# An encoder trunk on eight cores: the tail of the retention group norm is reordered, and half of the state's bf16 copies move to GpSimd

## What is computed

```python
def step(state, qkv):                       # one chunk, one direction
    qi, ki, vi = qkv
    scores = jnp.einsum('bhid,bhjd->bhij', qi, ki) * intra_decay
    out = jnp.einsum('bhij,bhjv->bhiv', scores, vi)
    out = out + jnp.einsum('bhid,bhdv->bhiv', qi * q_decay, state)
    state = state * chunk_decay + jnp.einsum('bhjd,bhjv->bhdv', ki * k_decay, vi)
    return state, out
...
o = o_fwd + o_bwd
o = o - jnp.mean(o, axis=-1, keepdims=True)                       # group norm, per token and head
o = o * lax.rsqrt(jnp.mean(o * o, axis=-1, keepdims=True) + NORM_EPS)
return (jax.nn.silu(g) * o.astype(x.dtype)) @ w_o
```

## Time and profile before

| | us |
|---|---|
| two runs | 4858.53 and 5156.21, median 5007.37 |
| the profiled execution | 4702.69 |
| its span, slowest core (7) | 4701.6 |
| spans of all cores | 4670.8 to 4701.6 |
| mean granted TensorE clock of the cores | 0.916 to 0.923 |
| busy, core 7: PE / DVE / ACT / POOL | 3935.8 / 1492.5 / 1539.7 / 1039.7 |

### The profile page before, as it was taken

One profiled execution on the slowest core, in us unless ns is written; L12 is line 12 of the kernel. 1 busy time (PEld: TensorE's weight loads), 2 busy tenths in 40 slices (PEclk: granted clock), 3 DMA queues, 4 the chain that ended last, 5 costly groups with the idle time before them and its releaser, 6 DMA issues.

```text
span 4701.6 us, 57281 instructions; the slowest of 8 cores (4670.8 to 4701.6 us)
## 1 busy us (share of the span) xinstructions
PE 3935.8 (84%) x17553; PEld 1719.2 (37%) x17553; DVE 1492.5 (32%) x2537; ACT 1539.7 (33%) x2739; POOL 1039.7 (22%) x946
## 2 busy tenths in 40 slices
PE   3666798999989999999867678879798897978879
PEld 2222343443434444444323233334343343433334
DVE  3102324334242525243243042341513324142341
ACT  2111233433242433334234134152432515144141
POOL 3121020202112020202133223212322222223122
PEclk8778898999999999999978899999999999999999
DMA  9999856455454545445698953344434444444333
GB/s 133 148 151 170 187 161 177 168 176 161 171 179 163 187 155 191 162 170 166 194 207 165 160 174 124 144 148 153 157 118 171 127 154 145 137 159 132 135 110 126
DMA packets 262929, 742.01 MB, mean 158 GB/s; under 512 B 105950, under 2 KB 144862, under 8 KB 204268
## 3 DMA queue, kind: packets, MB, share of 16 engines
q1 hardware_dynamic: 132172, 679.63, 44.5%
q0 software_dynamic: 130464, 58.73, 12.9%
HBM read 692.16 MB, written 163.58 MB: 182 GB/s over the span
## 4 chain that ended last, share of the span: by engine, by line
PE 64%; issue 8%; DVE 7%; DMA 7%; ACT 6%; another core or an unknown queue 4%; POOL 3%; SPq 0%; DVEq 0%; ACTq 0%; POOLq 0%
PE bank L427 46%; PE bank L653 5%; PE bank L725 4%; DMA sb_wring<-wscr 4%; PE bank L886 3%; ACT sb_Sbf L575 2%; DVE sb_xn L419 1%; PE bank L413 1%; DVE sb_misc L948 1%; PE bank L566 1%; DMA wscr<-w_down 1%; PE bank L943 1%; POOL sb_hm L855 1%; PE bank L939 1%
## 5 line engine op out<-in xcount | busy, mean ns | idle before, releaser
L427 PE MATMUL bank<-sb_xn,sb_wring 128*128 128x512 bf16 x5120 | 1254.4, 403 | 199.5 <-DVE sb_xn L419 75.1
L427 PE MATMUL bank<-sb_hm,sb_wring 128*128 128x512 bf16 x4608 | 1021.9, 384 | 59.2 <-DMA sb_wring<-wscr 26.6
L451 POOL TENSOR_TENSOR sb_hm<-sb_rstd 128x512 bf16<-128x512 f32 x512 | 529.5, 1039 | 1705.8 <-ACT sb_rstd L450 1704.1
L427 PEld LDWEIGHTS bank<-sb_xn,sb_wring 128*128 128x128 bf16 x5120 | 516.1, 102 | 924.5 <-issue 419.7
L427 PEld LDWEIGHTS bank<-sb_hm,sb_wring 128*128 128x128 bf16 x4608 | 454.6, 99 | 623.2 <-issue 96.7
L450 ACT ACTIVATE sb_rstd<-bank 128x512 f32<-128x512 f32 x512 | 302.5, 596 | 762.4 <-PE bank L427 581.5
L653 PE MATMUL bank<-sb_xn,sb_wring 128*128 128x512 bf16 x1536 | 375.9, 403 | 42.8 <-DMA sb_wring<-wscr 29.4
L569 DVE SCALAR_TENSOR_TENSOR sb_S<-sb_S,bank 128x512 f32<-128x512 f32 x512 | 312.5, 679 | 301.3 <-PE bank L566 289.3
L403 ACT ACTIVATE sb_xn<-sb_xT 128x512 bf16<-128x512 f32 x224 | 134.8, 629 | 621.1 <-DVE sb_xT L463 424.3
L463 DVE TENSOR_TENSOR sb_xT<-bank,sb_xT 128x512 f32<-128x512 f32 x96 | 66.4, 691 | 767.0 <-PE bank L427 767.0
L575 ACT CAST sb_Sbf<-sb_S 128x512 bf16<-128x512 f32 x512 | 292.3, 618 | 29.4 <-DVE sb_S L569 14.5
(11 more groups left out here) (168 smaller groups left out, 3020.3 us busy)
## 6 DMA issues: line engine op xcount, KB each, us to landing
sb_wring<-wscr SPq DMA_DIRECT2D x400, 1024.0 KB, 5.8
sb_wring<-wscr SPq DMA_DIRECT2D x64, 768.0 KB, 5.7
sb_scr<-sb_Sbf SPq DMA_DIRECT2D x32, 1024.0 KB, 8.8
sb_kvA<-sb_scr SPq DMA_DIRECT2D x128, 256.0 KB, 3.7
sb_xin<-x SPq DMA_DIRECT2D x32, 512.0 KB, 10.3
wscr<-w_up POOLq DMA_DIRECT2D x16, 1024.0 KB, 94.1
wscr<-w_down POOLq DMA_DIRECT2D x32, 512.0 KB, 37.2
x_scr<-sb_xT SPq DMA_DIRECT2D x8, 2048.0 KB, 7.8
```

The costliest lines, as they stand in the source:

```text
L427: PE.op(lambda: nc.tensor.matmul(bk[:], slab[:, k * C + mm * 128:k * C + (mm + 1) * 128], rhs[k], start=(k == 0), stop=(k == KC - 1)), rea ...
L451: POOL.op(lambda: nc.gpsimd.tensor_tensor(hm_k[j], rt, rt, ALU.mult), reads=[rstd_R[rb]], writes=[HR[j]])
```

## The change

Three things. The group norm of a head is finished at once, in the loop, and not one head later. The shift nm is computed in two steps: DVE negates the mean (nmn, by a tensor_scalar of one column) right behind the aggregate, and ACT multiplies it with rs (an Identity activation with a pointer scale); rs and nm now have a region of their own, `misc_R[8 + h]`. And in pass 2 `state_update` gives the casts of dc = 1 (odd i) to POOL; pass 1 keeps all on ACT.

```diff
--- before.py
+++ after.py
@@ -558,7 +558,7 @@
                   reads=[rot_R[2], rot_R[3]], writes=[rot_R[2]])
             emit2(rot[:, 2, :], rot_R[2])
 
-        def state_update(n, kt, ktR, vt_c, vt_cR, gC, sbuf_i, boundary, grp="main"):
+        def state_update(n, kt, ktR, vt_c, vt_cR, gC, sbuf_i, boundary, grp="main", split_copy=False):
             for h in range(4):
                 for dc in range(2):
                     i = h * 2 + dc
@@ -572,8 +572,12 @@
                     if boundary:
                         DVE.op(lambda: nc.vector.tensor_scalar(S[:, i, :], S[:, i, :], flag_ap, None, ALU.mult),
                                reads=[S_R[i], R_const], writes=[S_R[i]])
-                    ACT.op(lambda: nc.scalar.copy(Sbf[:, sbuf_i, i, :], S[:, i, :]),
-                           reads=[S_R[i]], writes=[Sbf_R[sbuf_i][i]])
+                    if split_copy and dc == 1:
+                        POOL.op(lambda: nc.gpsimd.tensor_copy(Sbf[:, sbuf_i, i, :], S[:, i, :]),
+                                reads=[S_R[i]], writes=[Sbf_R[sbuf_i][i]])
+                    else:
+                        ACT.op(lambda: nc.scalar.copy(Sbf[:, sbuf_i, i, :], S[:, i, :]),
+                               reads=[S_R[i]], writes=[Sbf_R[sbuf_i][i]])
 
         GCF = [math.exp(128.0 * LGF[h]) for h in range(4)]
         GCB = [math.exp(128.0 * LGB[h]) for h in range(4)]
@@ -913,22 +917,6 @@
                        reads=[bsR, R_const], writes=[PT_R[pb]])
                 gb_ = c % 2
                 STAGE[0] = "P2.ret.o"
-                obanks = []
-
-                def gn_finish(h, c=c, gb_=gb_, obanks=obanks):
-                    bo, boR = obanks[h]
-                    ag = misc[:, 32 + 4 * h:32 + 4 * h + 2]
-                    rs_ = misc[:, 32 + 4 * h + 2:32 + 4 * h + 3]; nm = misc[:, 32 + 4 * h + 3:32 + 4 * h + 4]
-                    mR = misc_R[h]
-                    DVE.op(lambda: nc.vector.scalar_tensor_tensor(nm, ag[:, 0:1], -1.0, rs_, ALU.mult, ALU.mult),
-                           reads=[mR], writes=[mR])
-                    ob = h % 2
-                    ACT.op(lambda: nc.scalar.activation(on_[ob], bo[:], AF.Identity, bias=nm, scale=rs_),
-                           reads=[boR, mR], writes=[rot_R[ob]])
-                    POOL.op(lambda: nc.gpsimd.tensor_tensor(gated[:, 4 * gb_ + h, :], on_[ob],
-                                                            gact[:, c, h * 512:(h + 1) * 512], ALU.mult),
-                            reads=[rot_R[ob], gact_R[c][h]], writes=[gated_R[gb_][h]])
-
                 for h in range(4):
                     bo, boR = bank("o")
                     PE.op(lambda: nc.tensor.matmul(bo[:], PTb[:, h * 128:(h + 1) * 128], v2[:, h * 512:(h + 1) * 512],
@@ -942,21 +930,26 @@
                         m = 2 * h + dc
                         PE.op(lambda: nc.tensor.matmul(bo[:], qb_k[m][:, cs_], sbl[:, m, :], start=False, stop=(dc == 1)),
                               reads=[qb_R[m], sbl_R[h]], writes=[boR], signal=(dc == 1))
-                    st = misc[:, 8 * h:8 * h + 6]; ag = misc[:, 32 + 4 * h:32 + 4 * h + 2]
-                    rs_ = misc[:, 32 + 4 * h + 2:32 + 4 * h + 3]
-                    mR = misc_R[h]
+                    st = misc[:, 8 * h:8 * h + 6]; nmn = misc[:, 8 * h + 6:8 * h + 7]
+                    ag = misc[:, 32 + 4 * h:32 + 4 * h + 2]
+                    rs_ = misc[:, 32 + 4 * h + 2:32 + 4 * h + 3]; nm = misc[:, 32 + 4 * h + 3:32 + 4 * h + 4]
+                    mR = misc_R[h]; mR2 = misc_R[8 + h]
                     DVE.op(lambda: nc.vector.bn_stats(st, bo[:]), reads=[boR], writes=[mR])
                     DVE.op(lambda: nc.vector.bn_aggr(ag, st), reads=[mR], writes=[mR])
-                    ACT.op(lambda: nc.scalar.activation(rs_, ag[:, 1:2], AF.Ln, bias=EPS, scale=1.0), reads=[mR], writes=[mR])
-                    ACT.op(lambda: nc.scalar.activation(rs_, rs_, AF.Exp, scale=-0.5), reads=[mR], writes=[mR])
-                    obanks.append((bo, boR))
-                    if h >= 1:
-                        gn_finish(h - 1)
-                gn_finish(3)
+                    DVE.op(lambda: nc.vector.tensor_scalar(nmn, ag[:, 0:1], -1.0, None, ALU.mult), reads=[mR], writes=[mR])
+                    ACT.op(lambda: nc.scalar.activation(rs_, ag[:, 1:2], AF.Ln, bias=EPS, scale=1.0), reads=[mR], writes=[mR2])
+                    ACT.op(lambda: nc.scalar.activation(rs_, rs_, AF.Exp, scale=-0.5), reads=[mR2], writes=[mR2])
+                    ACT.op(lambda: nc.scalar.activation(nm, rs_, AF.Identity, scale=nmn), reads=[mR, mR2], writes=[mR2])
+                    ob = h % 2
+                    ACT.op(lambda: nc.scalar.activation(on_[ob], bo[:], AF.Identity, bias=nm, scale=rs_),
+                           reads=[boR, mR2], writes=[rot_R[ob]])
+                    POOL.op(lambda: nc.gpsimd.tensor_tensor(gated[:, 4 * gb_ + h, :], on_[ob],
+                                                            gact[:, c, h * 512:(h + 1) * 512], ALU.mult),
+                            reads=[rot_R[ob], gact_R[c][h]], writes=[gated_R[gb_][h]])
                 if n + 1 < NCH:
                     ret_loads_sb(n + 1)
                 STAGE[0] = "P2.ret.st"
-                state_update(n, kf2, kf2_R, v2, v2_R, GCF, 0, boundary=(n == 15), grp="r")
+                state_update(n, kf2, kf2_R, v2, v2_R, GCF, 0, boundary=(n == 15), grp="r", split_copy=True)
                 STAGE[0] = "P2.ret.gT"
                 for half in range(2):
                     bk, bR = bank("r")
```

## The result

| | before | after |
|---|---|---|
| median of all runs | 4763.96 us (32 runs, 4686.15 to 5274.12) | 4671.67 us (33 runs, 4657.04 to 5218.8) |
| profiled execution | 4702.69 us | 4674.73 us |
| span of the slowest core | 4701.6 us | 4673.7 us |

The ratio of the undisturbed runs is 0.9945, with a 95% interval of 0.9927 to 0.9962; in part of the executions of either kernel the cores of one die run at a lower granted clock and the time is up to 12% longer, so the medians of all runs mix two levels and the ratio doesn't. The change gains 0.55%, about 26 us; the profiled executions differ by 28.0 us. That is far from 2%, and clear of no change.

What follows compares the result with a forecast made beforehand. Bound: a chain over four engines in pass 2's retention chunks. Eight tiles at 1.5 us give 12, slow-clock chunks 3.5, tile 0 hides 1: about 15 us, 4702.69 to 4688 profiled, scaled 5007.37 to 4991; range 4690 to 5110.

Steps and rivals of the forecast that it cites:

- part (3): Plain chunk: nmn3 waits for gate1 on POOL through the shared port; updates start at T 7.70, chunk 13.53 us, 0.34 gained.
- rival A: nmn does not wait for POOL: plain chunk 13.14 us, 0.73 gained; 27 us in all, 4676 profiled; chance 0.23.
- The chain: Plain chunk's period: updates from T 8.04, 4.79 to the next mask, 1.04 to the next matmul, sum 13.87 us.
- the casts: State casts on ACT: the next chunk does not wait for them, except in the last chunk of a tile.
- part (1): Norm of each head: nm moves to ACT as an Identity with pointer scale, taken as a step of 0.40 us.
- part (4): After gate3, ending T 10.93, next chunk's scores are ready some T 12.1 against 12.49 on DVE's side, covered by 0.4.
- part (5): Four of eight state casts go to POOL: 0.7 us each, all in time, worth nothing in a plain chunk.
- rival C: Slower: POOL copies bind from 1.7 us each; at 2.2 us plain chunk 14.6, 5034 us in all; chance 0.09.
- part (6): Last chunk of a tile: wo projection starts at T 13.75 instead of 14.68, 0.93 us gained on ACT.
- part (7): First chunk of a tile: overlap hiding its table load is lost; updates at 8.97 against 8.81, 0.1 to 0.2 us lost.
- part (8): Chunk at lower clock: updates at about T 8.75 instead of 9.79, 1.0 us gained; five such chunks give 3.5 more.
- Tile 0: First tile: PE waits 21 us for a load there, which hides 1 us of the gain.

## Why the prediction was right or wrong

The sign was right, and so was that the change stays within 2%. Two steps failed: the low end of the range, so that the measured median lies outside it, and the port wait of part (3). The change gained 26 to 28 us where the sum had 15; of the 11 to 13 between them, part (3) makes some 8 (0.32 us in each of 16 plain chunks, 0.33 in each of 8 last ones), the first chunks 1, the clock 2 to 3.

- **The range failed by its scale.** I carried the forecast over in proportion to the median of the two runs then shown, 5007.37 us. Over 32 runs the median before is 4763.96, and the two runs both lie well above it. In proportion to the profiled execution the forecast was 4688, rival A 4676; measured were 4674.73 profiled and 4671.67 in the median. The low end of 4690 lay above even my own sum for the profiled execution: with a profile that had run 6% faster than the median, the low end had to go below that sum.
- **The port wait, part (3), failed.** I let nmn3 wait for gate1, since the 512-column operation did. It doesn't wait, in any of the 52 of 128 cases in which it starts beside a gate. The runs with two columns and with two inputs show what does wait, and that even then I had mis-sized the term: 0.12 us a chunk, not 0.56. Of the 0.44 between them, 0.24 is that the unheld updates start at T 7.38 and not 7.14, with nmn3 at 7.21 and not 7.04, when gate1 (T 6.40 to 7.55) is nearly over; 0.20 is that behind a held nmn3 they start at 7.5 and not 7.70. So of the 0.32 by which a plain chunk came out shorter than forecast, 0.12 is the wait that wasn't there, and 0.20 its length.
- **Rival A had the right mechanism** (chance given 0.23): 0.73 a plain chunk there, 0.66 measured; 27 us in all there, 26 measured by the ratio. That the sums agree so well is in part luck. It had the updates at T 7.1 and the mask waiting for the scores; they start at 7.38, and at full clock the mask doesn't wait. It had 0.25 for the first chunk and 1.45 for the last, where 0 and 1.26 came out, and the clock made up for that.
- **The chain, and the casts, held.** 4.79 and 1.04 are unchanged; with the split undone the plain chunk doesn't move, and with the split alone it doesn't either.
- **nm on ACT, part (1), held, at its upper end.** It takes 0.294 us, and from its start to the apply's are 0.44 us where I had 0.40. With it head 3 came at 4.71 (4.62 forecast). The rest of the 0.24 is 0.07 from PE to the statistics and 0.07 to the first update.
- **What is late next, part (4), was close.** In a plain chunk of after at full clock the mask finds the scores ready, 0.24 us ahead of it in the chunk shown (they end at 4486.62); at a lower clock it waits for them. With the updates made early the scores bind, as the run with four banks shows.
- **The copies on POOL, part (5), held:** 0.57 us each in a row (0.7 taken), all in time. The threshold of 1.7 is bracketed by 1.15 and 2.3. The price behind it was far above mine: rival C had a plain chunk of 14.6 at 2.2 us a copy, measured are 16.6 to 17.8 at 2.3.
- **The last chunk, part (6),** gained 1.26, not 0.93, since the updates were not held: rival A's 1.45 less the longer steps.
- **The first chunk, part (7):** a loss of 0.1 to 0.2 was forecast. In tile 4 the median over the cores went from 14.62 to 14.80 and the updates from T 8.77 to 8.96 (8.97 forecast), and over seven tiles the mean is unchanged. Head 3 came at 5.92 (5.90 forecast). But the hit is in part luck: nmn3 isn't held here either (0.15 us); instead the statistics of head 3 come 1.5 to 1.9 behind its first matmul in tile 4 (1.4 to 1.6 before, 1.34 forecast), since the matmuls between them run in part at a lower clock (two take up to 1.06 us instead of 0.59). The gain that rival A had here, without the wait, didn't come.
- **Clock, part (8).** At full clock the chain gives 2 x 0.66 + 1.26 = 2.6 us a tile, 18 over seven tiles, and chunk 15's extra 5.8 us became 5.5. The seven tiles lost 25.3 on core 7 and 23.8 in the mean of the cores. So some 18 us are the chain's, and 5 to 7 come from fewer or cheaper chunks at the lower clock. I had 0.7 more for each of five such chunks, 3.5. That the shorter idle times bring it isn't shown: with the split alone some 5 us beyond the last chunks came too, at unchanged plain chunks, and in the four-bank run the clock fell.
- **Tile 0** gave nothing on core 7; there the load is the bound. I had taken off 1 us for this, and left it 0.5.

## What to carry to other kernels

Lay a stage's chain out by one period and check that its parts add up to the period before pricing a change: here the 4.79 from the first update to the mask and the 1.04 to the next matmul held wherever the scores were ready, and a longer distance showed that the other chain had taken over. Two edits that each cut one of two nearly equal chains give little or nothing alone and much together, and an edit that takes a wait off one engine may only pay with the order that another engine needs for it; try such edits in pairs. And when the level of the times is uncertain, let the range reach below the sum for the fastest execution seen.

## What the runs showed of the hardware

- A DVE operation that starts beside a POOL tensor_tensor was held to within 0.03 us of its end if it had two SBUF inputs (scalar_tensor_tensor of one column, up to 1.06 us instead of 0.16) or was a tensor_scalar of two columns (up to 1.04 instead of 0.17); a tensor_scalar of 512 columns took 1.47 instead of 0.49 beside one. Not held were a tensor_scalar of one column (0.153 to 0.156 us in all 128 cases, 52 of them beside a gate), the aggregate (six columns in, two out, 0.181 to 0.183), and the state updates, which read PSUM and one SBUF tensor (0.60 a step). The Trainium skill ("SBUF — State Buffer", Who interferes with whom) says that DVE shares a port pair with GpSimd, that two SBUF inputs or a 2-port mode make it contend, and that tensor_scalar is of the operations that can enter such a mode. The traces agree with it; they show what is held, not the mode.
- A dependent ACT step with a pointer scale costs 0.44 us up to the next dependent start, against 0.30 without; the operation itself 0.294 against 0.203.
- POOL casts 128x512 from f32 to bf16 in 0.61 us, 0.57 in a row, half of its tensor_tensor's 1.16.
